# GpSimd takes over the softmax scaling of a block attention, and a strided operand is laid out densely

## What is computed

```python
c = k.reshape(B, G, T // CMP_STRIDE, CMP_STRIDE, dh)
blocks = jnp.concatenate([c[:, :, :-1], c[:, :, 1:]], axis=3) + pos
flat = blocks.reshape(B, G, blocks.shape[2], CMP_BLK * dh)
return jax.nn.gelu(flat @ w1) @ w2
```

## Time and profile before

| | us |
|---|---|
| median of 3 timed runs | 3132.75 |
| lowest and highest of them | 3125.09, 3135.55 |
| the profiled execution's own time | 3136.32 |
| its span, first to last instruction | 3134.3 |
| PE busy | 3074.6 (98%) |
| POOL busy | 1902.8 (61%) |
| DVE busy | 1501.1 (48%) |
| ACT busy | 724.1 (23%) |

### The profile page before, as it was taken

The page is one execution under the profiler, slowest core; times in us unless marked ns, Lnnn a source line. Parts: engine busy times, 40 slices in busy tenths (PEclk is TensorE's granted clock), DMA queues, the critical chain, the costliest instruction groups (busy, mean ns, idle before and its releaser), DMA issues.

```text
span 3134.3 us, 41325 instructions
## 1 busy us (share of the span) xinstructions
PE 3074.6 (98%) x15116; PEld 2466.4 (79%) x15116; DVE 1501.1 (48%) x2613; ACT 724.1 (23%) x1461; POOL 1902.8 (61%) x885
## 2 busy tenths in 40 slices
PE   8999999999999999999999999999999999999998
PEld 6688888868888888877688888888887668888887
DVE  4654520455552143886645455214388664545411
ACT  4410100441100123434601110012343550111000
POOL 4277778437777876001288777787700128877776
PEclk9999999999999999999999999999999999999999
DMA  3132333213333322112033333332211203233222
GB/s 124 48 108 98 97 95 100 75 34 108 101 94 95 100 87 88 48 35 81 21 94 94 101 99 95 95 100 88 87 48 35 81 22 100 94 101 94 100 94 87
DMA packets 71713, 262.29 MB, mean 84 GB/s; under 512 B 8208, under 2 KB 8208, under 8 KB 71440
## 3 DMA queue, kind: packets, MB, share of 16 engines
q1 hardware_dynamic: 71280, 258.34, 25.9%
q10 hardware_dynamic: 288, 1.98, 0.2%
HBM read 258.20 MB, written 2.10 MB: 83 GB/s over the span
## 4 chain that ended last, share of the span: by engine, by line
PE 85%; DVE 6%; issue 4%; POOL 3%; ACT 2%; DMA 0%; DVEq 0%; POOLq 0%; SPq 0%; ACTq 0%
PE bank L642 83%; POOL w_hi L1408 1%; POOL w_lo L1416 1%; PE bank L1272 1%; DVE arena L1983 1%; DVE bank L1983 1%; DVE rope L1983 1%; PE bank L657 0%; DVE arena L2354 0%; DVE rope L1980 0%; ACT act_hi L1563 0%; ACT arena L1905 0%; DVE w_lo L2380 0%; DVE x L1983 0%; ACT bank L1562 0%
## 5 line engine op out<-in xcount | busy, mean ns | idle before, releaser
L1408 POOL TENSOR_TENSOR w_hi<-ring,one 128x1024 fp32r<-128x1024 f32 x430 | 818.7, 1904 | 1160.9 <-PE bank L642 578.4
L1416 POOL TENSOR_TENSOR w_lo<-ring,w_hi 128x1024 fp32r<-128x1024 f32 x422 | 1039.0, 2462 | 40.3 <-DVE h_lo L2007 7.5
L642 PE MATMUL bank<-h_hi,w_hi 128*128 128x512 f32 x2256 | 893.9, 396 | 3.4 <-POOL w_lo L1416 3.4
L642 PE MATMUL bank<-h_hi,w_lo 128*128 128x512 f32 x2256 | 879.6, 390 | 0.0
L642 PE MATMUL bank<-h_lo,w_hi 128*128 128x512 f32 x2256 | 879.0, 390 | 0.0
L642 PE MATMUL bank<-act_hi,w_hi 128*128 128x512 f32 (+1 forms) x1376 | 507.2, 395 | 6.1 <-POOL w_lo L1416 2.7
L642 PEld LDWEIGHTS bank<-h_hi,w_hi 128*128 128x128 f32 x2256 | 423.1, 188 | 97.0 <-issue 5.4
L642 PEld LDWEIGHTS bank<-h_hi,w_lo 128*128 128x128 f32 x2256 | 423.0, 187 | 90.9
L642 PEld LDWEIGHTS bank<-h_lo,w_hi 128*128 128x128 f32 x2256 | 423.4, 188 | 84.9 <-issue 1.0
L642 PE MATMUL bank<-act_hi,w_lo 128*128 (+1 forms) x1120 | 438.2, 391 | 0.0
L642 PE MATMUL bank<-act_lo,w_hi 128*128 (+1 forms) x1120 | 420.9, 390 | 1.4 <-DVE act_lo L2574 1.4
(11 more groups left out here) (248 smaller groups left out, 2863.6 us busy)
## 6 DMA issues: line engine op xcount, KB each, us to landing
ring<-wstream SPq DMA_DIRECT2D x480, 512.0 KB, 3.5
par<-params SPq DMA_DIRECT2D x4, 529.5 KB, 4.3
x<-xT SPq DMA_DIRECT2D x4, 512.0 KB, 7.2
outT<-h SPq DMA_DIRECT2D x4, 512.0 KB, 2.7
cst<-const ACTq DMA_DIRECT2D x1, 1412.0 KB, 8.9
par<-params ACTq DMA_DIRECT2D x1, 525.5 KB, 5.2
arena<-pos SPq DMA_DIRECT2D x1, 256.0 KB, 2.6
cst<-const SPq DMA_DIRECT2D x1, 24.5 KB, 2.4
```

The source lines that it names most:

```text
L642: return pe.matmul(out, lhsT, rhs, start=start, stop=stop)
L1408: return po.tensor_tensor(out, a, one.broadcast_to([P, n]), ALU.mult)
L1416: po.tensor_tensor(pair_[1], raw, pair_[0].bitcast(F32), ALU.subtract).then_inc(done.sem, 1)
```

## The change

Four edits.

1. `pair_scale` moves from VectorE to GpSimd and is done step by step. VectorE keeps a small part (`pair_factor`): the reciprocal and the multiply with the gate for the two columns of one step. It stands behind the mask of the step two later, so behind the mask of step s + 2 for step s. GpSimd has a new `pair_scale(w, t)`: it waits for the factor and scales the two pieces of the step; after the fourth step it raises the signal that TensorE's turn waits for.
2. On GpSimd the splitting of merge tile 2 goes behind all 32 scalings.
3. The two-input multiply `times_one` becomes a one-input `tensor_scalar` by 1.0 (`rounded`), for all high halves that GpSimd makes (422 of 128x1024 in `w_hi`, and the few others); the column of ones, its memset and its semaphore go. GpSimd's loops over layers and tiles are written out instead of looped.
4. `cv` and `ck` are laid out by residue: token 16 b + r is kept at place 32 r + b. The moving operand of `hidden` is then three runs of 31 neighbouring floats. ScalarE's copy `nvc` and VectorE's two multiplies of `rope(0)` write with a step of 32 floats, the shift by one token becomes one by 32 places, and the two small copies of biases get other patterns. TensorE's instructions are the same in number and order.

```diff
-        ns_w = later(at_w, 16)
+        ns_w = later(at_w, 64)
...
+        def by_residue(a):
+
+            return a.rearrange("p (r b) -> p b r", r=16)
...
+                        at = p % 8 * 2 * (T // 16) + p // 8
                         last = product(b[:, 0:3 * NCMP], ring[:, t % RING, (p % 8) * P:(p % 8) * P + P],
-                                       data[:, :, 2 * p:2 * p + 16 * (NCMP - 1) + 1:16], p == 0, p == 15)
+                                       data[:, :, at:at + NCMP], p == 0, p == 15)
...
-            def times_one(out, a, n):
-
-                return po.tensor_tensor(out, a, one.broadcast_to([P, n]), ALU.mult)
+            def rounded(out, a):
+
+                return po.tensor_scalar(out, a, 1.0, None, ALU.mult)
...
-                    elif i == 2:
-                        po.wait_ge(*ns_c(l, 2))
...
-                for i in range(NMERGE + ND):
+                def pair_scale(w, t):
+
+                    po.wait_ge(*ns_w(l, 2 * (NT * w + t) + 2))
+                    for e in range(2):
+                        v = nprob[w % 3][e][:, PS0[t]:PS0[t] + (t + 1) * P]
+                        c = 32 + 8 * (w % 2) + 4 * e + t
+                        last = po.tensor_scalar(v, v, small[:, c:c + 1], None, ALU.mult)
+                    if t == NT - 1:
+                        last.then_inc(ns_c.sem, 1)
+
+                split_merge(0)
+                split_merge(1)
+                for w in range(8):
+                    for t in range(NT):
+                        pair_scale(w, t)
+                for i in range(2, NMERGE + ND):
                     split_merge(i)
...
-            with po.Fori(0, LAYERS) as l:
+            for l in range(0, LAYERS):
...
+                        if name == "nvc":
+                            last = sc.activation(by_residue(dst), by_token(b[:, :]), ACT.Copy)
...
-                ve.tensor_copy(cv[64:P, 0, 0:T - 1], cv[0:64, 0, 1:T]).then_inc(cv_o.sem, 1)
+                ve.tensor_copy(cv[64:P, 0, 0:T - NB], cv[0:64, 0, NB:T]).then_inc(cv_o.sem, 1)
...
+                    if i == 0:
+                        mul(by_residue(ropes), by_token(rotation_bank(0)[:, :]), by_token(C("sin2"))).then_inc(rp_p.sem, 1)
+                        mul(by_residue(ropec), by_token(raw_block(0)), by_token(C("cos2"))).then_inc(rp_p.sem, 1)
...
-                def pair_scale(w):
-
+                def pair_factor(step):
+
+                    w, t = step // NT, step % NT
                     j, win = pair(w)
-                    ve.wait_ge(*ns_e(l, NT * (w + 1)))
...
+                    ve.wait_ge(*ns_e(l, step + 1))
+                    if w >= 2 and t == 0:
+                        ve.wait_ge(*ns_c(l, w - 1))
+                    c = 8 * (w % 2) + t
+                    inv = small[:, 32 + c:40 + c:4][:, 0:2]
+                    ve.reciprocal(inv, small[:, 16 + c:24 + c:4][:, 0:2]).then_inc(ns_w.sem, 1)
+                    ve.wait_ge(*ns_w(l, 2 * step + 1))
+                    mul(inv, inv, gates[:, 2 * j:2 * j + 2, t, 1 + win]).then_inc(ns_w.sem, 1)
...
-                    if w >= 1:
-                        pair_scale(w - 1)
...
+                        if step >= 2:
+                            pair_factor(step - 2)
                         if w >= 2 and step == NT * w + 3:
                             last_turned(w - 2)
                     if w == 8:
+                        pair_factor(30)
+                        pair_factor(31)
                         last_turned(6)
```

More of the change, by code:

```diff
@@ L123, in build @@
         w_lo = sb("w_lo", [P, 2, TILE], F32R)
-        one = sb("one", [P, 1])
         bank = [ctx.enter_context(nc.psum_tensor(f"bank{i}", [P, T], F32)) for i in range(8)]
@@ L446, in build, with by_token @@
         LIN_PLACED = {hd: 10 * (hd + 1) for hd in range(4)} | {4: 59, 5: 60, 6: 79, 7: 80}
+        def by_residue(a):
+            return a.rearrange("p (r b) -> p b r", r=16)
+        def by_token(a):
+            return a.rearrange("p (b r) -> p b r", r=16)
         def raw_block(i):
@@ L1405, in _ @@
         def _(po):
-            def times_one(out, a, n):
-                return po.tensor_tensor(out, a, one.broadcast_to([P, n]), ALU.mult)
+            def rounded(out, a):
+                return po.tensor_scalar(out, a, 1.0, None, ALU.mult)
             def halves(raw, pair_, high, count, done, clear=None):
-                times_one(pair_[0], raw, TILE).then_inc(high.sem, 1)
+                rounded(pair_[0], raw).then_inc(high.sem, 1)
                 po.wait_ge(high.sem, count)
@@ L1513, in ffn @@
                     split(s)
-                with po.Fori(0, 7) as it:
+                for it in range(0, 7):
                     for s in range(2, 8):
@@ L1518, in ffn @@
                     split(s)
-                with po.Fori(0, 3) as it:
+                for it in range(0, 3):
                     for s in range(46, 52):
@@ L1525, in _ @@
             po.sem_inc(w_split.sem, w_split.start)
-            po.memset(one[:, :], 1.0).then_inc(s_one, 1)
-            po.wait_ge(s_one, 1)
-            with po.Fori(0, LAYERS) as l:
+            for l in range(0, LAYERS):
                 mixer1(l)
                 ffn(l, l, 0, MIX1_TILES, PER1)
-            with po.Fori(0, LAYERS) as l:
+            for l in range(0, LAYERS):
                 mixer2(l)
@@ L1745, in copy_out @@
                                "nvc": m2["cv"][:, 0, :]}[name]
-                        last = sc.activation(dst, b[:, :], ACT.Copy)
+                        if name == "nvc":
+                            last = sc.activation(by_residue(dst), by_token(b[:, :]), ACT.Copy)
+                        else:
+                            last = sc.activation(dst, b[:, :], ACT.Copy)
                     last.then_inc(y_out.sem, 1)
@@ L2442, in rope @@
                         ve.wait_ge(*rp_o(l, (4, 5, 6, 7, 8, 12)[i - 1]))
[L2443 to L2444 removed]
+                    if i == 0:
+                        mul(by_residue(ropes), by_token(rotation_bank(0)[:, :]), by_token(C("sin2"))).then_inc(rp_p.sem, 1)
+                        mul(by_residue(ropec), by_token(raw_block(0)), by_token(C("cos2"))).then_inc(rp_p.sem, 1)
+                    else:
+                        mul(ropes, rotation_bank(i)[:, :], C("sin2")).then_inc(rp_p.sem, 1)
+                        mul(ropec, raw_block(i), C("cos2")).then_inc(rp_p.sem, 1)
                     ve.wait_ge(*rp_p(l, 2 * i + 2))
@@ L2510, in mixer2 @@
                 cmp_norm(3)
-                def pair_scale(w):
+                def pair_factor(step):
+                    w, t = step // NT, step % NT
                     j, win = pair(w)
-                    ve.wait_ge(*ns_e(l, NT * (w + 1)))
-                    c = 8 * (w % 2)
-                    inv = small[:, 32 + c:40 + c]
-                    ve.reciprocal(inv, small[:, 16 + c:24 + c]).then_inc(ns_w.sem, 1)
-                    ve.wait_ge(*ns_w(l, 2 * w + 1))
-                    inv2 = inv.rearrange("p (e m) -> p e m", e=2)
-                    mul(inv2, inv2, gates[:, 2 * j:2 * j + 2, :, 1 + win]).then_inc(ns_w.sem, 1)
-                    ve.wait_ge(*ns_w(l, 2 * w + 2))
-                    for e in range(2):
-                        for t in range(NT):
-                            v = nprob[w % 3][e][:, PS0[t]:PS0[t] + (t + 1) * P]
-                            last = ve.tensor_scalar(v, v, small[:, 32 + c + 4 * e + t:33 + c + 4 * e + t], None, ALU.mult)
-                    last.then_inc(ns_c.sem, 1)
+                    ve.wait_ge(*ns_e(l, step + 1))
[6 more added lines that the diff above has]
+                    mul(inv, inv, gates[:, 2 * j:2 * j + 2, t, 1 + win]).then_inc(ns_w.sem, 1)
                 def last_turned(w):
```

20 lines of the change are left out of this document (11 added, 9 removed).

## The result

| | before | after |
|---|---|---|
| median of the timed runs, us | 3134.15 (4 runs) | 3210.72 (4 runs) |
| lowest and highest | 3125.09, 3136.57 | 3208.96, 3213.16 |
| after over before, 95% interval | | 1.0239 (1.0220 to 1.0257) |
| span of the profiled execution | 3134.3 | 3210.3 |

The account below looks back on a forecast made before the run. TensorE's own work was taken to bound the kernel (busy 98% of 3134.3 us). Compression -6.1, high halves -5.5, scaling +2.4 and clock -1.4 gave -10.6 us: a median of 3122 us, range 3111 to 3137.

Parts of the forecast that it names:

- the part on edit 3: GpSimd's high halves: 1.4 us each instead of 1.92, closing TensorE's gaps for -5.5 us, ends 0 and about 10.
- One input is no cheaper: Rival, 20%: GpSimd's cost is per column, not per input, so the one-input high halves give nothing; 3129 us.
- GpSimd has time over: Feed-forward window: GpSimd busy 39.6 of 50 us, so faster GpSimd instructions count only where TensorE stands still for them.
- Compression: 128 TensorE passes of 93 columns in the second kind of layer: 0.112 us instead of 0.160 each, -6.1 us.
- The hand-overs: Four hand-overs to the feed-forward part: high half ends 0.5 us earlier, TensorE's 0.84 us gap shrinks; -2.0, at most 3.4.
- The gaps of 0.69 and 0.95 us in the second kind: Last low part ahead of `w_out`, 1.0 us gained, at most 1.4; norm at the start, 0.5 for both layers.
- Tile 2 of `w_out` and the linear attention: TensorE's gaps of 1.36 us (first kind) and 2.65 us (linear attention), twice each: 1.0 us gained at each, at most 2.1.
- The scaling: Attention: scalings go to GpSimd, factors stay on VectorE's queue; 1.2 us a layer, +2.4 in all, ends 0 and +8.
- the slow rival: Rival, 10%: VectorE's factor multiplies stand still beside GpSimd's scalings, 24 to 31 us over 14 attention rounds; 3146 us.
- The clock: Clock falls at the gaps at 1257.7 and 1100.3, 1.4 us lost each; half counted as gone, -1.4 us.
- One input is cheap: Rival, 17%: a high half near 1.0 us closes gaps to their bounds, 9 instead of 5.5 us; 3117 us.
- the four rivals: One input is cheap, One input is no cheaper, the slow rival, and three separate runs costing, not the step (8%, 3128).

Follow-up runs that it names:

- the run with one place slow: Changed kernel, but in the feed-forward parts only place 0 of `w_hi` keeps the one-input high half, place 1 has the two-input multiply; 3209.75 us, ratio 1.0236.
- e10: The changed kernel with `tensor_scalar` by 1.0 for the high halves replaced by a copy; 3123.59 us, ratio to before 0.9959.
- e9: The kernel before with the layout by residue, GpSimd's loops written out and all high halves made by a copy; 3117.03 us, ratio 0.9942.
- the first experiment: The changed kernel with only the high halves taken back to the two-input multiply with the column of ones; 3136.43 us, ratio 1.0006.
- e11: The kernel before with the layout by residue and GpSimd's loops written out, high halves still by the two-input multiply; 3136.72 us, ratio 0.9993.

## Why the prediction was wrong, step by step

**The step that failed** is the price of the high half in the part on edit 3: "The nearest rows: the same work with two inputs, 1.92, above, and VectorE's one-input operation, 0.43 for 512 columns, so 0.86 for 1024, below". The upper end was taken from the instruction that is being replaced, on the belief that one input less can't cost more. No row excluded that: "with 0 and 1.06 as ends" has no end on the side of a loss. It measured 2.80. So the term of the sum for edit 3, -5.5, was mis-sized past its ends: edit 3 alone measured a ratio of 1.0239, some +75 us. The rival "One input is no cheaper" stopped at the same point. The rule of the Trainium skill that the prediction weighed, "GPSIMD Engine Reference" (Elementwise — side-by-side cycle accounting), one element a cycle for one input, was an estimated 1.0 us. The trace agrees with it for a copy, 1.04, and not for `tensor_scalar`, 2.80.

**The second failure** made the first one costly: "GpSimd has time over", from 39.6 busy us of 50. The idle time was real, 1.07 us a tile. But it was not room for a dearer high half: 0.47 us of it was. The rest is the time in which a place isn't free yet and GpSimd can do nothing. The round of a place (passes, release, high, low, release) can be read off the trace of before, and a rival built on it could have said: at 1.9 + 0.9 us, half of 0.4 us for each tile ahead of which GpSimd waits for TensorE (376 now, 393 before), some 75 us. From the run with only the high halves taken back to the changed kernel, the start of GpSimd's same high halves drifts apart by 12.3 to 12.9 us in each feed-forward part, 50 of some 82 us. Of the rest, 6.4 us come between 100 and 117 us, where the changed kernel's profiled execution ran at the lower clock, and the other 26 or so grow in the mixers, which use the same two places. A part of these is clock too: over the span the two executions lost 30.2 and 17.9 us of full-speed time to it. That helps to explain why their spans differ by 82 and the medians by 74 us.

The other steps:

- *Compression*, -6.1. The passes came as forecast: 3.70 and 3.81 us a group, 1.6 less, four groups -6.2; 0.110 us a pass, where 0.112 was said. In the timed runs it is -0.13% with a wide interval, and the falls of the clock behind it (the run of edit 4 alone) were not in the sum.
- *The hand-overs*, gap 0.84 to 0.3. They closed altogether, and not for the reason given. At the second feed-forward tile the step from the pass before is 0.32, 0.26, 0.26 and 0.23 us, where it was 1.22 or 1.23. The high half didn't end earlier, but VectorE hardly stood still beside it: `h_lo` took 1.10 us and ended in the middle of it, where it took 1.88 in the earlier trace rows.

```profile
1785.14 2.77 POOL L1415 TENSOR_SCALAR w_hi<-ring 128x1024 fp32r<-128x1024 f32 x1 [0.46 <-PE bank L648]
...
1785.62 1.10 DVE L2028 SCALAR_TENSOR_TENSOR h_lo<-x,par,h_hi 128x512 fp32r<-128x512 f32 x1
...
1790.32 0.39 PE L648 MATMUL bank<-h_hi,w_lo 128*128 128x512 f32 x1
1790.58 0.50 PE L648 MATMUL bank<-h_hi,w_hi 128*128 128x512 f32 x1
```

  In the layers of the first kind a new gap of 0.31 and 0.32 us stands one tile earlier. The gaps of 0.69 and 0.95 us in the second kind went to 0.04 and under 0.15. With the next item, the gaps that the -5.5 was made of lost some 4 to 5 us together. That this is near the forecast is luck, since the high halves got dearer and not cheaper.

- *Tile 2 of `w_out` and the linear attention.* Where the tile itself is waited for, the dearer half is paid in full: 1.36 became 2.25. The gap of 2.65 shrank to 0.42, and a new one of 1.59 behind the late low half took its place.

```profile
160.75 0.50 PE L648 MATMUL bank<-act_hi,w_hi 128*128 128x512 f32 x1 [2.25 <-POOL w_lo L1423]
...
1281.87 1.10 PE L648 MATMUL bank<-arena,rope 128*128 128x64 f32 x8 [0.42 <-DVE rope L2001]
...
1289.13 0.50 PE L648 MATMUL bank<-h_hi,w_hi 128*128 128x512 f32 x1 [1.59 <-POOL w_lo L1423]
```

- *The scaling.* GpSimd's pieces were forecast at 0.4, 0.6, 0.8, 1.05 and took 0.60, 0.92, 1.24, 1.56 us, 8.7 a pair instead of 5.7: the same wrong price. It was kept harmless by the reserve that the prediction had worked out (a column may cost 2.6 ns; it costs 2.5): the turns of group 0 are 8.2 and 9.2 us apart as before. Round 7 has its new gap, 0.73 us in the changed kernel (forecast 0.8). The first round's gap was forecast at 1.1 and is 1.02 with the two-input high halves, but 1.85 in the changed kernel:

```profile
1494.08 2.35 POOL L1423 TENSOR_TENSOR w_lo<-ring,w_hi 128x1024 fp32r<-128x1024 f32 x1
...
1495.45 1.00 DVE L2001 TENSOR_TENSOR small<-small,arena 128x2 f32<-128x2 f32 x1
...
1497.74 1.20 PE L648 MATMUL bank<-arena 64*128 64x256 f32 x4 [1.85 <-DVE small L2578]
```

  The factor's multiply of two columns stood still for 0.84 us until the low half of merge tile 1 ended, since the high halves had pushed that low half into the first round. This is the mechanism of the slow rival, at one place in each layer instead of in 14 rounds. The granted clock falls behind it, to 0.66 in this window:

```profile
1497.00:1502.00 5.00, 4.26 (x13) 2.99 (x14) 2.62 (x20) 3.27 (x12) 4.69 (x6) 0.66 0.32 108
```

  Such a fall costs 1.7 us. It follows all four gaps of 1.85 us (two here, two in the run with one place slow), and none of the 22 gaps of 0.74 or 1.02 at this place in the other kernels. The scaling as a whole is e10 against e9, and the kernel of the first experiment against e11: +0.17% and +0.13%, 4 to 5 us where +2.4 was forecast. Neither difference is well outside its uncertainty.
- *The clock*, -1.4. Of the two falls that it weighed, the one behind the gap at 1100.3 is gone in the changed kernel's profiled execution and the one behind 1257.7 is still there, though that gap shrank. That is the half that was said, but it shows little: the run of edit 4 alone lacks the first fall too, with nothing done to its gap. The new falls above were not in the sum.
- *The rivals.* "One input is cheap", 3117, happens to be the time of e9 with its copy, which has a high half near 1.0 us but not the scaling on GpSimd. With the scaling (e10) it is 3124. None of the four rivals contained the case that came.

## What to carry to other kernels

A bound for an operation that the trace doesn't show is not the operation that it replaces: on GpSimd, measure the form itself, in one kernel with a few forms side by side, before it goes into the inner loop 422 times. Where two engines pass tiles round through a small number of places, the reserve is not the idle time of the feeding engine but places x tile time minus one full round of a place; read that round off the timeline first. A stall of 0.2 us a tile doesn't show in shares of busy time and hardly in a list of waits: count the passes in a window, or compare the starts of the same instruction in both traces.

## What the runs showed of the hardware that was not expected

- GpSimd's price for 128x1024 from float32 to the rounded type: copy 1.04 us, multiply by a spread column 1.90, subtract of two full inputs 2.40, `tensor_scalar` 2.77 to 2.86. One input and one scalar is the dearest of the four. In float32 in place, `tensor_scalar` has the same slope: (1562 - 602) / 384 = 2.5 ns a column.
- VectorE's operations with two SBUF inputs stand still beside GpSimd's two-input operations and the copy, and much less beside `tensor_scalar`. So the rule that the prediction quoted behind its last rival, exclusion for a whole instruction, fits the first two and not the third. `h_lo` beside the copy in e9 ends 0.55 us after the copy's end, as it did beside the multiply in the earlier trace rows; beside `tensor_scalar` it ends 1.2 us before that. It isn't free of it altogether: alone it takes 0.73, beside `tensor_scalar` 1.10. VectorE's busy time fell from 1501 to 1190 us by the change, some 39 of them the scalings (1214 with edit 3 alone), and the kernel was slower all the same.

```profile
190.42 1.04 POOL L1417 CAST w_hi<-ring 128x1024 fp32r<-128x1024 f32 x1 [1.59 <-PE bank L650]
...
190.93 1.08 DVE L2019 SCALAR_TENSOR_TENSOR h_lo<-x,par,h_hi 128x512 fp32r<-128x512 f32 x1
```

- It works the other way too: a low half of GpSimd that starts while VectorE's `act_lo` is under way takes 2.73 us instead of 2.39.
